# Two transformer blocks, fp32, on one core: the second layer's modulation in three places instead of one

## What is computed

```
c_act = silu(c)
for layer in range(2):
    mod = (c_act @ ada_w[layer] + ada_b[layer])[:, None, :]
    sh1, sc1, g1, sh2, sc2, g2 = jnp.split(mod, 6, axis=-1)
    h = rms_norm(x, norm1_g[layer]) * (1.0 + sc1) + sh1
    mix = even_mixer(h, ...) if layer % 2 == 0 else odd_mixer(h, ...)
    x = x + g1 * mix
    h = rms_norm(x, norm2_g[layer]) * (1.0 + sc2) + sh2
    x = x + g2 * grouped_moe(h, router_w, router_b, exp_w_gate[layer], ...)
```

## Time and profile before

| what | us |
|---|---|
| time, median of 3 runs | 2347.82 |
| lowest, highest | 2340.65, 2353.23 |
| the profiled execution's own time | 2347.66 |
| its span, first to last instruction | 2345.9 |
| mean granted TensorE clock in it | 0.984 |

### The profile page before, as it was taken

How to read it: one execution, slowest core, us unless ns; L and a number is a source line. 1 busy time by engine, 2 the same in 40 slices (tenths; PEclk the granted TensorE clock), 3 DMA queues, 4 the chain that set the end, 5 groups by cost and what they waited for, 6 DMA issues and landing times.

```text
span 2345.9 us, 33848 instructions
## 1 busy us (share of the span) xinstructions
PE 2248.5 (96%) x14476; PEld 1895.6 (81%) x14476; DVE 1526.1 (65%) x1499; ACT 1125.5 (48%) x1213; POOL 69.2 (3%) x128
## 2 busy tenths in 40 slices
PE   6998999989999999999999999998999999999999
PEld 4777888767787799877778899787888788887887
DVE  5767889678855655798866564546656566545655
ACT  4344334467646433577654455334444544435443
POOL 2030010000000000000000000000000000020000
PEclk9999999899999999999999999999999999999999
DMA  9854999789842265799855552003555565533553
GB/s 346 328 184 149 330 320 322 246 301 379 306 144 90 77 230 170 252 366 365 303 178 187 188 174 87 2 4 127 197 198 179 170 199 180 179 96 101 186 185 121
DMA packets 261111, 477.64 MB, mean 204 GB/s; under 512 B 8465, under 2 KB 150897, under 8 KB 257633
## 3 DMA queue, kind: packets, MB, share of 16 engines
q1 hardware_dynamic: 251264, 431.81, 53.5%
q0 software_dynamic: 9696, 43.66, 5.5%
HBM read 473.30 MB, written 2.14 MB: 203 GB/s over the span
## 4 chain that ended last, share of the span: by engine, by line
PE 82%; DVE 8%; ACT 5%; DMA 4%; issue 1%; POOL 0%; SPq 0%; ACTq 0%; DVEq 0%; POOLq 0%
PE psum L1006 14%; PE psum L1008 7%; PE psum L1023 3%; PE psum L1025 3%; PE psum L1024 3%; PE psum L974 3%; PE psum L976 3%; PE psum L975 3%; DVE w_lo L2631 3%; PE psum L1390 2%; PE psum L1392 2%; PE psum L1391 2%; PE psum L1305 2%; PE psum L1306 2%; PE psum L1307 2%; PE psum L1422 2%
## 5 line engine op out<-in xcount | busy, mean ns | idle before, releaser
L2631 DVE TENSOR_TENSOR w_lo<-ring,w_hi 128x2048 fp32r<-128x2048 f32 x320 | 730.5, 2288 | 290.6 <-ACT w_hi L2016 289.0
L2016 ACT ACTIVATE w_hi<-ring 128x2048 fp32r<-128x2048 f32 x320 | 612.0, 1915 | 384.0 <-PE psum L1025 119.8
L1006 PE MATMUL psum<-h_both,w_hi 128*128 128x512 f32 x1408 | 499.4, 399 | 1.6 <-DVE h_both L3292 1.3
L1008 PE MATMUL psum<-h_both,w_lo 128*128 128x256 f32 x1408 | 395.1, 281 | 0.0
L1006 PEld LDWEIGHTS psum<-h_both,w_hi 128*128 128x128 f32 x1408 | 264.5, 188 | 68.1 <-issue 1.7
L1008 PEld LDWEIGHTS psum<-h_both,w_lo 128*128 128x128 f32 x1408 | 265.9, 189 | 1.4
L2631 DVE TENSOR_TENSOR w_lo<-pool,w_hi 128x2048 fp32r<-128x2048 f32 x65 | 148.8, 2290 | 48.7 <-ACT w_hi L2016 48.0
L2038 ACT ACTIVATE pool<-psum 128x512 f32<-128x512 f32 x88 | 52.6, 598 | 261.2 <-PE psum L1008 261.2
L1390 PE MATMUL psum<-w_hi,h_both 128*128 128x512 f32 x384 | 156.9, 409 | 8.1 <-DVE w_lo L2631 7.9
L2016 ACT ACTIVATE w_hi<-pool 128x2048 fp32r<-128x2048 f32 x65 | 124.6, 1917 | 69.3 <-PE psum L1392 17.1
L1392 PE MATMUL psum<-w_lo,h_both 128*128 128x512 f32 x384 | 151.3, 394 | 0.0
(11 more groups left out here) (457 smaller groups left out, 3977.8 us busy)
## 6 DMA issues: line engine op xcount, KB each, us to landing
ring<-in_exp_w_down SPq DMA_DIRECT2D x48, 1024.0 KB, 7.4
ring<-in_exp_w_gate SPq DMA_DIRECT2D x47, 1024.0 KB, 6.5
ring<-in_ffn_pre_w_in SPq DMA_DIRECT2D x44, 1024.0 KB, 5.1
ring<-in_ffn_post_w_in SPq DMA_DIRECT2D x44, 1024.0 KB, 5.1
ring<-in_exp_w_up SPq DMA_DIRECT2D x32, 1024.0 KB, 7.0
pool<-in_exp_w_up SPq DMA_DIRECT2D x32, 1024.0 KB, 7.7
ring<-in_ada_w SPq DMA_DIRECT2D x24, 1024.0 KB, 7.1
pool<-in_ada_w POOLq DMA_DIRECT2D x32, 768.0 KB, 6.6
```

The lines of the kernel that those rows point to most:

```text
L1006: pe.matmul(o.rearrange("p (s n) -> p s n", s=2), wh[:, k, fs], h_both[:, :, k, :], start=k == 0, stop=False, skip_group_check=True)
L1008: m = pe.matmul(o[:, 0:T], wl[:, k, fs], h_hi[:, k, :], start=False, stop=k == KD - 1, skip_group_check=True)
L2016: act.activation(w_hi[:, (s["split"] + r) % 3, :], piece(s["pieces"][r]), ACT.Copy)\
L2631: dve.tensor_tensor(w_lo[:, slot, :], piece(s["pieces"][r]), w_hi[:, slot, :].bitcast(F32), ALU.subtract).then_inc(sem("w_lo"), 1)
```

## The change

The six parts of the second layer are made in four stages (`ADA_ROWS`), each of which goes over the eight rows of `ada_w[1]`, in parts of 128 x 1024:

- parts 0 and 1 (shift and scale of the odd layer's norm) and then part 2 (the first gate) in the first experts' wide steps: 16 + 8 transfers of 512 KB, three VectorE parts a step in place of four of 1536;
- parts 3 and 4 (shift and scale before the second experts) beside the odd gemm: 8 transfers of 1 MB, two parts each (`ada1_pairs`, three buffers), two VectorE parts for each of eight pieces (`beside_odd`); the first pair is loaded in the first experts, the next two around the odd layer's norm;
- part 5 (the second gate) in the second experts: 8 transfers of 512 KB, two parts in each of four wide steps.

The sums lie elsewhere (`ada_sums`), so `PROJ` is free and `moe0` uses the extra slots from its first piece. On TensorE, 16 of the 32 column products stay in expert 1; 16 are spread over six turns of the odd attention; the first gate row is made in the turn of pair 6 there, and ScalarE copies it (1024 columns at once) at the start of `gemm("odd_out")`, before which VectorE waits for it; the second gate row is made in wide step 6 of the second experts. The column biases come with `gain_cols` and are added by VectorE. Semaphores are merged (`routed`, `rw_prepared`), with no other effect.

```diff
+ADA_ROWS = [(0, 1), (2,), (3, 4), (5,)]
...
-    p.moe("moe0", ("egate", MOD_AT + 6, 0), ("mod_rows", 6))
+    p.moe("moe0", ("gate", 0, 0))
...
-        acc = view(PROJ, ADA_W)
+        ada_sums = [view(ROWS + 2048, 2 * D), view(WORK + 8192, D), view(ROWS, 2 * D), view(ROWS, D)]
...
+            for n in range(ADA_ENDS[1], ADA_ENDS[2], 2):
+                first = (n - ADA_ENDS[1]) // 2
+                if first == 0:
+                    pl.wait_ge(sem("mod_cols"), 3)
+                elif first == 1:
+                    pl.wait_ge(sem("norm_xn"), 2 * NORMS.index("n_odd") + 2)
+                elif first == 2:
+                    pl.wait_ge(sem("h_split_lo"), SPLIT_BASE["n_odd"] + SPLITS["n_odd"])
+                else:
+                    pl.wait_ge(sem("ada1_used"), n - 4)
+                ada_load_pair(n)
...
+                    if layer == 1 and c == ROW_AT:
+                        pe.wait_ge(sem("side_act"), 10)
+                        pe.wait_ge(sem("side_dve"), 10)
+                        gate_row_1(3, 6)
...
-                    if layer == 0 and MOD_AT <= e < MOD_AT + 5:
-                        modulation_1(e - MOD_AT)
+                    if layer == 0 and e == MOD_AT:
+                        pe.wait_ge(sem("wide_in"), 1)
+                        modulation_1(0, lambda i: bank(3)[:, i:i + 1], range(2 * KD))
...
-                    pe.wait_ge(sem("sb_weights"), p + 1)
                     if p > 1:
                         pe.wait_ge(sem("h_split_lo"), SPLIT_BASE["odd_mix"] + p - 1)
...
+                    if 1 <= p <= 6:
+                        turn_, first = (p - 1) // 2, KD * (p % 2)
+                        some = range(first + 3 * turn_, min(first + 3 * turn_ + 3, first + KD))
+                        modulation_1(2, lambda i: bank(6 + p % 2)[:, T + i:T + i + 1], some, turn_ == 2)
+                    if p == 6:
+                        pe.wait_ge(sem("sb_exp"), 6)
+                        gate_row_1(1, 4)
+                    pe.wait_ge(sem("sb_weights"), p + 1)
...
+            def odd_out_first(c):
+                if c == 0:
+                    row_moved(3, 4)
+
+            gemm("odd_out", None, odd_out_first)
...
-            dve.wait_ge(sem("mod_rows_in"), 6)
             norm("n_odd")
...
+            def beside_odd(i):
+
+                if 1 <= i <= 8:
+                    ada_part(ADA_ENDS[1] + 2 * i - 2)
+                    ada_part(ADA_ENDS[1] + 2 * i - 1)
+
+            gemm("odd_in", None, odd_first, beside_odd)
...
+                    if p == 5 or p == 6:
+                        dve.wait_ge(sem("mod_cols"), p - 1)
...
+            dve.wait_ge(sem("mod_rows_in"), 3)
             gemm("odd_out")
```

More of the change, by code:

```diff
@@ L54 @@
 MOD_AT = 1
+ROW_AT = 6
 FFN_CHUNKS = DFF // HC
@@ L137, in __init__, with add @@
         self.gemm_chunks = self.swi_chunks = self.split = 0
-    def add(self, kind, what, free, slot=None, first=None):
+    def add(self, kind, what, free, slot=None):
         s = self.slot if slot is None else slot
         self.loads[s] += 1
-        self.pieces.append(dict(kind=kind, what=what, slot=s, after=[self.held[s], first], landed=16 * self.loads[s]))
+        self.pieces.append(dict(kind=kind, what=what, slot=s, after=[self.held[s]], landed=16 * self.loads[s]))
         self.held[s] = free
@@ L212, in moe @@
             if n >= wide and turn < EXTRA:
-                self.add(kind, (name, c, half), ("w_lo", self.split), RAW + turn, first)
+                self.add(kind, (name, c, half), ("w_lo", self.split), RAW + turn)
             else:
```

176 lines of the change are left out of this document (102 added, 74 removed).

## The result

The changed kernel takes 2327.05 us (median of 4 runs, 2323.15 to 2329.75), the kernel before 2350.31 us in the same comparison (4 runs, 2340.65 to 2353.23): a ratio of 0.9909, 95% interval 0.9886 to 0.9933, faster by 0.9%. The forecast was 2324 us, 23.5 us less; between these medians lie 23.3 us, between the two profiled executions (2347.66 and 2327.66 us) 20.0.

A forecast was written before the change was run, and what follows sets the result against it. TensorE was taken as the bound, busy 2248.5 of 2345.9 us. Terms -34.8 + 5.4 + 0 + 0.5 + 2.1 + 1.6 + 1.7 = -23.5 us took 2347.7 to 2324 us, range 2313 to 2339.

The forecast's parts named there:

- The slots, -34.8 for the whole: First experts, first wide gate product to last scatter: the whole 34.8 us excess over the second experts goes.
- the three named causes: First experts: extra slots missing until the seventh expert, 32 column products (11.52 us) at low clock, four row products (3.4 us).
- Rival A: First experts: slots not the cause of slow transfers, some 17 us of waiting stays; -6, 2342 us; chance 7%.
- the 32 modulation parts in the wide steps: First experts' wide steps: 58 us of VectorE parts cost nothing because TensorE is full; replacing them with 31 us gives 0.
- The 16 columns, +5.4: First experts, behind expert 1: 16 remaining column products cost 3.6 us plus 1.8 for the clock; bounds 3.6 and 7.
- First pair, odd gemm: 0: First pair's load hidden, at most 2.9 us; odd gemm keeps 5.77 us a piece, VectorE at 5.2, bound 4 us.
- Rival C: Odd gemm bound by its pairs once landing exceeds 14.3 us; slower kernel at some 28 us, 2360 us; chance 3%.
- The rule that speaks against the pairs: Odd gemm: GpSimd-issued transfers stall while VectorE takes the shared port, so pairs could be late; the prediction went by measured landings.
- Attention, +0.5 and +2.1: Odd attention: three column products a turn fill a 0.69 us wait, +0.5 in six turns; gate row unhidden, +2.1.
- Rival B: Odd attention: one-column products let the clock fall and stay low for six turns, +18, 2342 us; chance 6%.
- Output gemm, +1.6: Output gemm: VectorE waits for ScalarE's row copy before splitting piece 1, so TensorE waits 1.6 us; bounds 0 and 2.5.
- Second experts, +1.7: Second experts: the gate row's two products stand in a full TensorE without cover, +1.7 us; VectorE parts and loads 0.

The follow-up runs named there:

- late slots: Changed kernel with the three extra slots used in the first experts only from expert 7 on; also called the first experiment: 2340.68 us, ratio 0.9981.
- the second 16 columns: Changed kernel with the 16 column products between experts 1 and 2 made twice over, so 32 stand there: 2331.50 us, ratio 0.9943.
- the fitted kernel: Changed kernel, first gate row before the last down products, column products split 4, 4, 3, 5 over TensorE's waits (expert 3 to odd norm): 2316.34 us, ratio 0.9869.
- the doubled parts: Changed kernel with one more 1024-column VectorE operation, result unused, beside each of the 16 modulation parts in the odd gemm: 2331.82 us, ratio 0.9947.
- six products a turn: Changed kernel with the 16 column products in the odd attention made twice over, six a turn in place of three: 2329.60 us, ratio 0.9934.
- the run with both moves: Changed kernel with the 16 column products at the first experts' end and the first gate row before their last down products: 2316.04 us, ratio 0.9876.
- the one with less filler: Kernel with columns fitted to TensorE's waits and gate row early, with 14 in place of 18 filler products in the second router: 2314.86 us, ratio 0.9871.

## Why the prediction came out right, point by point

**The slots, -34.8 for the whole.** The stretch came down to 365.9 us (364 forecast), the waits for transfers are gone from ScalarE's rows, and late slots brought them back. That the sum was taken whole from the second experts was right; that the three named causes are all of it was not, nor the split that Rival A and the first experiment used. Late slots cost 13.9 us, the second 16 columns 6.6, the first 16 up to 6.7, the four row products 3.4 (not tested by themselves): 30.6 of 34.8.

The rest has a fourth cause, which the prediction had put at nothing: the 32 modulation parts in the wide steps. The first turn of the sparse experts (L1403, now L1447) shows where it lies. Here are the first and the second experts of the kernel before, then the changed kernel and late slots:

```profile
L1403 PE MATMUL psum<-keep,pool x48: 270/272/275, 421.7 to 639.2; 128*128 128x128 f32 x48
...
L1403 PE MATMUL psum<-keep,pool x48: 270/272/273, 981.4 to 1172.3; 128*128 128x128 f32 x48
```

```profile
L1447 PE MATMUL psum<-keep,pool x48: 270/272/275, 413.3 to 610.9; 128*128 128x128 f32 x48
```

```profile
L1447 PE MATMUL psum<-keep,pool x48: 270/272/273, 410.9 to 621.2; 128*128 128x128 f32 x48
```

From the first wide gate product to this turn it is 167.9 us before, 159.7 in the second experts, 160.0 in the changed kernel and only 161.3 with late slots. So 8.2 of the 34.8 us lie before any column product, and late slots bring back 1.3 of them. TensorE was full to the end of the wide steps, as the prediction read, but VectorE and the transfers were behind: the last part was still being waited for when TensorE was in the sparse steps, and the splits stood behind it in VectorE's queue (kernel before, VectorE and TensorE):

```profile
408.05 1.82 DVE L2971 SCALAR_TENSOR_TENSOR pool<-pool,cact 128x1536 f32<-128x1536 f32 x1 [0.59 <-DMA pool<-in_ada_w]
```

```profile
414.48 0.47 PE L1390 MATMUL psum<-w_hi,h_both 128*128 128x512 f32 x1 [3.95 <-DVE w_lo L2631]
```

TensorE waited 6.0 us for splits between 385 and 425, and its clock was 0.72 from 415 to 421; late slots, with lighter parts and the same three slots there, has 2.0 us of waits. Whether VectorE's 58 us or the 25 MB of loads weighed more, no run separates. From the first turn to the last it is the other way: late slots cost 12.7 us there, the second 16 columns 6.9, the first 16 6.7, the rows 3.4, together 29.7 us, but the stretch was only 217.5 - 190.9 = 26.6 us longer than in the second experts, so these costs overlap.

**The 16 columns, +5.4.** The one term that was clearly too small: from the first turn (L1447) to the last it is 197.6 us in the first trace and 190.9 in the fitted kernel, so 6.7 us; the five other traces with the columns in that place and early slots have 195.9 to 197.6, so 5.0 to 6.7. The working gave 1.8 us for the clock, from a low stretch of 4 us at the start of the kernel; here it was 6.2 us long. Its upper bound of 7 held. A second slip changes nothing: 2319 us less 0.3% is 2312, where the working has 2314 for its best case.

**First pair, odd gemm: 0.** Right. No part waited for its pair, the pace stayed 5.76 us, the seven loads landed after 5.0 to 6.2 us, far from the 14.3 at which Rival C would begin. VectorE's load was a little under the 5.2 us a piece of the working (37.89 us busy from 650 to 694, 5.0 a piece); that it is close to the bound, the doubled parts showed. The rule that speaks against the pairs, in the Trainium skill (SBUF — State Buffer, Who interferes with whom), did not bite: its page limits it to VectorE operations that take the shared port, and the loads landed as fast (4.9 to 5.4 us) when VectorE had no idle time at all.

**Attention, +0.5 and +2.1.** The turn did not lengthen by 0.1 but by nothing, and six products a turn showed that this was cover and not slack elsewhere. The row took 1.96 us and the output gemm began 2.3 us later against the last scores, where 2.2 were due there. Rival B didn't come: the clock over the attention is 1.00.

```profile
707.00:741.00 34.00, 31.44 (x238) 26.19 (x240) 17.48 (x27) 22.98 (x32) 0.00 (x0) 1.00 0.00 1
```

**Output gemm, +1.6.** The mechanism was right to the row (split, split, copy, then VectorE at 746.67), the size 0.98 us: the working let TensorE begin with ScalarE, and it began 0.33 us later and took 5.7 us for the first piece.

**Second experts, +1.7.** 2.1 us in the trace.

**What the sum didn't have.** 2.4 us behind the second experts, from the granted clock in stages that the change doesn't touch. The prediction allowed 0.3% for differences between executions and that covers it, but it did not say where they arise. The agreement of 23.5 with 23.3 us is in part luck: the traced executions lie 20.0 apart, the spread between executions is larger than the agreement, and part of the 34.8 us came from a cause that the prediction had ruled out and still got because it took the difference whole.

## What to carry to other kernels

Where a stage has a twin in the same program, lay the two side by side by landmarks before pricing single instructions; the whole difference is then safe, its split into causes is not. A stage in which TensorE is full can still leave work and transfers behind for the next one: look at the first waits after it. Small products cost TensorE least where they fill a wait that the trace shows, in a number that fits the wait; in one row in a full stretch they also cost the clock behind them. When a gain of one or two microseconds shows up at one landmark and is gone at the next, look for filler work in a queue ahead of something that is waited for.

## What the runs showed of the hardware that was not expected

In code that the kernels share, nearly all of the difference between traces sits in a few short places where TensorE has gaps, and there the granted clock falls in one execution and not in the next. Over 14 traces:

| stretch, full work alike | shortest | longest |
|---|---|---|
| start to the first wide gate product (13 traces of the changed code) | 249.0 | 256.7 |
| 18 filler products in the second router (13 traces) | 4.13 | 7.05 |
| RWKV stage, first L1616 to last L928 | 34.3 | 43.0 |
| from there to the last L1869 | 110.4 | 113.1 |

The shortest and the longest of the third row, in the windows of the run with both moves and of the one with less filler:

```profile
1425.80:1460.10 34.30, 31.50 (x206) 27.07 (x206) 25.30 (x40) 14.96 (x30) 0.00 (x0) 0.90 0.00 1
```

```profile
1427.70:1470.70 43.00, 40.46 (x206) 34.55 (x206) 25.67 (x40) 15.19 (x30) 0.00 (x0) 0.70 0.00 0
```

The same 206 TensorE instructions took 31.5 us at a clock of 0.90 and 40.5 us at 0.70. By the Trainium skill (TensorE: Matmul & The Clock Gate, What's actually happening) the number of products at the low clock differs between runs of one kernel and is worth under 1% of a typical span (it says so of the first products of a kernel). These traces agree, with up to 8.7 us, 0.4%, in one stage, and show that the same goes on in the middle of a kernel. A stage in which TensorE is nearly full, the second experts (194.64 of 199.00 us busy behind the wide steps), agreed to 0.3 us in all 13 traces of the changed code (360.9 to 361.2).

Also new: one-column products are not alike at the two clocks in a mixed row. 16 took 3.94 us, the next 16 in the same row 6.8 us. And VectorE's first part of a sum, a plain product with a scalar, took 0.75 us for 1024 columns where the multiply-and-add takes 1.28; the working had 1.28 for both.
